# First output projection of a two-layer kernel, computed by column halves around the turn of the state-space result

## What is computed

```python
def even_layer(h, ...):                       # h: 512 tokens x 1024
    ...
    attn = rmsnorm(diff_attention(...), subln_w) * (1.0 - lambda_init)
    y_a = attn.reshape(b, s, 1024) * silu(g_a)
    ...
    y = ssd_scan(xh, dt, A, bm, cm)           # chunks of 128 tokens, 2 groups of 8 heads
    y = (y + xh * d_skip[:, None]).reshape(b, s, 1024) * silu(z)
    y_b = rmsnorm(y in 2 groups of 512, ssd_norm_w)
    return concatenate([y_a, y_b], -1) @ w_out   # w_out: 2048 x 1024
x = x + even_layer(rmsnorm(x, norm_a), ...)
x = x + odd_layer(rmsnorm(x, norm_c), ...)
```

## Time and profile before

| | |
|---|---|
| median of 3 executions | 1669.97 us (1668.33 to 1672.4) |
| the profiled execution's own time | 1672.1 us |
| its span, from the first to the last instruction | 1670.2 us |
| PE busy | 1575.8 us, 94% |
| DVE, ACT, POOL busy | 808.7, 655.9, 244.5 us |
| mean granted PE clock | 0.976 of full |

### The profile page before, as it was taken

How to read it: one execution, slowest core, us unless ns; L and a number is a source line. 1 busy time by engine, 2 the same in 40 slices (tenths; PEclk the granted TensorE clock), 3 DMA queues, 4 the chain that set the end, 5 groups by cost and what they waited for, 6 DMA issues and landing times. The chain is left out here.

```text
span 1670.2 us, 20830 instructions
## 1 busy us (share of the span) xinstructions
PE 1575.8 (94%) x7924; PEld 1287.3 (77%) x7924; DVE 808.7 (48%) x1600; ACT 655.9 (39%) x1324; POOL 244.5 (15%) x148
## 2 busy tenths in 40 slices
PE   7999999899799999998999999988998999999997
PEld 6888777687687879877878777767776888887886
DVE  4222288746723655526723477726654433333224
ACT  4222355552512467625235454453244322222212
POOL 0000022267400011120002223221200000000000
PEclk9999999999899999999999999988999999999999
DMA  5232211111232431122431221112220322322232
GB/s 203 101 102 88 89 51 51 39 51 47 80 101 77 132 102 39 39 84 87 141 96 64 89 70 57 51 52 76 89 76 26 101 90 100 101 89 92 96 100 76
DMA packets 39777, 137.60 MB, mean 82 GB/s; under 512 B 4928, under 2 KB 5312, under 8 KB 39552
## 3 DMA queue, kind: packets, MB, share of 16 engines
q1 hardware_dynamic: 34400, 125.32, 22.7%
q10 hardware_dynamic: 5280, 10.97, 2.2%
HBM read 128.02 MB, written 2.10 MB: 78 GB/s over the span
## 5 line engine op out<-in xcount | busy, mean ns | idle before, releaser
L210 ACT ACTIVATE cut_hi<-raw 128x1024 fp32r<-128x1024 f32 x228 | 241.6, 1060 | 646.8 <-PE ps L227 631.8
L227 PE MATMUL ps<-h_hi,cut_hi 128*128 128x512 f32 (+1 forms) x1120 | 453.0, 404 | 5.9 <-DVE h_lo L425 3.9
L215 DVE TENSOR_TENSOR cut_lo<-raw,cut_hi 128x1024 fp32r<-128x1024 f32 x172 | 211.8, 1231 | 492.0 <-ACT cut_hi L210 490.2
L229 PE MATMUL ps<-h_hi,cut_lo 128*128 128x512 f32 (+1 forms) x1120 | 438.1, 391 | 0.0
L228 PE MATMUL ps<-h_lo,cut_hi 128*128 128x512 f32 (+1 forms) x1120 | 437.8, 391 | 0.0
L227 PEld LDWEIGHTS ps<-h_hi,cut_hi 128*128 128x128 f32 x1120 | 212.5, 190 | 70.0 <-issue 22.9
L229 PEld LDWEIGHTS ps<-h_hi,cut_lo 128*128 128x128 f32 x1120 | 212.1, 189 | 45.6
L228 PEld LDWEIGHTS ps<-h_lo,cut_hi 128*128 128x128 f32 x1120 | 212.9, 190 | 37.6
L215 POOL TENSOR_TENSOR cut_lo<-raw,cut_hi 128x1024 fp32r<-128x1024 f32 x56 | 133.7, 2388 | 675.1 <-ACT cut_hi L210 675.1
L227 PE MATMUL ps<-cut_hi,h_hi 128*128 128x512 f32 (+1 forms) x368 | 143.4, 390 | 10.2 <-DVE cut_lo L215 6.4
L229 PE MATMUL ps<-cut_hi,h_lo 128*128 128x512 f32 (+1 forms) x368 | 142.5, 387 | 0.0
(11 more groups left out here) (312 smaller groups left out, 2103.3 us busy)
## 6 DMA issues: line engine op xcount, KB each, us to landing
raw<-weights SPq DMA_DIRECT2D x228, 512.0 KB, 3.3
scr<-scr ACTq DMA_DIRECT2D x34, 64.0 KB, 3.6
x<-x_in SPq DMA_DIRECT2D x4, 512.0 KB, 6.1
x<-x_in ACTq DMA_DIRECT2D x1, 2048.0 KB, 7.5
q_stack<-qT_lo ACTq DMA_DIRECT2D x16, 128.0 KB, 2.3
out<-x SPq DMA_DIRECT2D x4, 512.0 KB, 2.6
consts<-tables ACTq DMA_DIRECT2D x1, 1732.0 KB, 7.9
arena<-arena ACTq DMA_DIRECT2D x8, 128.0 KB, 2.3
```

What stands on the lines that cost most here:

```text
L210: act.activation(cut_hi[:, u % CUT, :], raw[:, u % RAW, :], ACT.Copy).then_inc(hi_ready, 1)
L215: eng.tensor_tensor(cut_lo[:, u % CUT, :], raw[:, u % RAW, :], cut_hi[:, u % CUT, :].bitcast(F32), ALU.subtract).then_inc(lo_ready, 1)
L227: a = pe.matmul(out, left[0], right[0], start=start, stop=False)
L229: return a, pe.matmul(out, left[1], right[0], start=False, stop=stop)
```

## The change

The parts TurnWaits, GroupMean, turn_a, TurnRead, GroupScale, turn_b, TurnDone and the Combine are replaced by one part, `OutA`, which does the same work in another order:

- The projection is made by column halves. The left 512 columns of all four token tiles need four banks (2, 3, 0, 1), the right 512 the other four (4 to 7). A weight unit now holds two 128-row blocks of one column half instead of one block of both; the host arranges it so. Units 0 to 7 are the left half, 8 to 15 the right.
- y_a is turned through the left banks in two rounds of four blocks. PE no longer waits for the whole scan first.
- The products of the left half start with y_a's blocks. At unit 3 PE turns y_b's blocks 0 to 3 through the right banks, at unit 4 blocks 4 to 7; the left half then goes on with y_b.
- DVE adds the left half to x in the middle of the part, and the right half at the end, with the norm's steps.
- The last two states (i = 6 and 7) are not made: no L1455 product, no weighted input, no forward step.

```diff
-        class TurnWaits(Part):
-
-
-            def pe(self, pe):
-                pe.wait_ge(sl_scaled, NT)
-                pe.wait_ge(y_out, 8)
-                pe.wait_ge(st_out, 8)
-                pe.wait_ge(segs_exp, 16)
-                pe.wait_ge(fill_g.out_act, 8)
...
         def squares_of(act, i):
             c, g = i // 2, i % 2
             act.wait_ge(z_scaled, i + 1)
-            act.wait_ge(st_out, i + 1)
+            if i < 6:
+                act.wait_ge(st_out, i + 1)
...
-                    pe.wait_ge(xdd_ready, i + 1)
-                    if i:
-                        pe.wait_ge(st_out, i)
-                    pe.matmul(ps[:, 6, :], b_tok[:, c, g * P:(g + 1) * P], xdd[i % 2], start=True, stop=True)\
-                      .then_inc(st_done, 1)
+                    if i < 6:
+                        pe.wait_ge(xdd_ready, i + 1)
+                        if i:
+                            pe.wait_ge(st_out, i)
+                        pe.matmul(ps[:, 6, :], b_tok[:, c, g * P:(g + 1) * P], xdd[i % 2], start=True, stop=True)\
+                          .then_inc(st_done, 1)
...
-                act.wait_ge(fill_g.out_act, 8)
-                turn_a.silus(act)
-                squares_of(act, 6)
-                squares_of(act, 7)
...
-                    if c > 0:
+                    if 0 < c < NT - 1:
...
+        class OutA(Part):
...
+            cuts = n - 1
+            after = None
+            left, right = (2, 3, 0, 1), (4, 5, 6, 7)
...
+            def turn(self, pe, y, k, bank, turned):
+                for t in range(NT):
+                    last = pe.transpose(ps[:, bank, t * P:(t + 1) * P], y[:, t, k * P:(k + 1) * P], ident)
+                last.then_inc(turned, 1)
...
+            def columns(self, pe, half, v, order):
+                w = None
+                for k, t in order:
+                    if w is None:
+                        w = unit(pe, self.u0 + v)
+                    y = [(h[:, k % 8, t * P:(t + 1) * P]) for h in ((h_hi, h_lo) if k < 8 else (yb_hi, yb_lo))]
+                    bank = (self.left, self.right)[half][t]
+                    if half == 0 and t == 0:
+                        pe.wait_ge(self.ya_lo_out if k < 8 else self.yb_lo_out, k % 8 + 1)
+                    if half == 0 and k == 0:
+                        pe.wait_ge(self.ya_gated, 4 + t + 1)
+                    if half == 1 and k == 0:
+                        pe.wait_ge(self.yb_lo_out, 4 + t + 1)
+                    a, z = product(pe, ps[:, bank, :], y, [h[:, (k % 2) * 512:(k % 2 + 1) * 512] for h in w],
+                                   k == 0, k == 15)
+                    if (k, t) == order[0]:
+                        first = a
+                    if k == 15:
+                        z.then_inc(self.done, 1)
+                return first
+
+            def pe(self, pe):
+                pe.wait_ge(sl_scaled, NT)
+                pe.wait_ge(fill_g.out_act, 8)
+                for k in range(4):
+                    if k == 2:
+                        pe.wait_ge(segs_exp, 16)
+                    self.turn(pe, y_a, k, self.left[k], self.ya_turned)
+                for k in range(4, 8):
+                    pe.wait_ge(self.ya_gated, k - 3)
+                    self.turn(pe, y_a, k, self.left[k - 4], self.ya_turned)
+                for v in range(8):
+                    if v == 3:
+                        pe.wait_ge(gs_scaled, 5)
+                        pe.wait_ge(gs_scaled_act, 3)
+                        pe.wait_ge(off_read, 6)
+                        pe.wait_ge(y_out, 8)
+                        pe.wait_ge(st_out, 6)
+                        for k in range(4):
+                            self.turn(pe, y_b, k, self.right[k], self.yb_turned)
+                    if v == 4:
+                        for k in range(4, 8):
+                            pe.wait_ge(self.yb_lo_out, k - 3)
+                            self.turn(pe, y_b, k, self.right[k - 4], self.yb_turned)
+                    self.columns(pe, 0, v, [(k, t) for k in (2 * v, 2 * v + 1) for t in range(NT)])\
+                        .then_inc(weights_used, 1)
+                for v in range(8, 14):
+                    self.columns(pe, 1, v, [(k, t) for k in (2 * v - 16, 2 * v - 15) for t in range(NT)])\
+                        .then_inc(weights_used, 1)
+                for t in range(NT):
+                    first = self.columns(pe, 1, 14, [(12, t), (13, t)])
+                    if t == 0:
+                        first.then_inc(weights_used, 1)
+                    first = self.columns(pe, 1, 15, [(14, t), (15, t)])
+                    if t == NT - 1:
+                        first.then_inc(weights_used, 1)
...
             def act(self, act):
-                act.wait_ge(turn_a.turned, 8)
+                act.wait_ge(fill_g.out_act, 8)
+                for k in range(8):
+                    act.activation(gate_a[:, k, :], gate_a[:, k, :], ACT.Silu).then_inc(self.ya_silued, 1)
+                    if k == 3:
+                        squares_of(act, 6)
+                squares_of(act, 7)
+                for k in range(8):
+                    if k == 6:
+                        cut_high(act, self.u0 + 1)
+                    act.wait_ge(self.ya_gated, k + 1)
+                    act.activation(h_hi[:, k, :], gate_a[:, k, :], ACT.Copy).then_inc(self.ya_hi_out, 1)
+                act.wait_ge(self.ya_turned, 8)
                 act.dma_start(x[:, :, :], x_dram.rearrange("(t p) d -> p t d", p=P)).then_inc(x_loaded, 16)
                 act.dma_start(big_row[:, :], big_dram[0, :].partition_broadcast(P)).then_inc(big_loaded, 16)
                 act.wait_ge(gs_rooted, 1)
                 for i in range(5, 8):
                     act.activation(groups_b[:, i, :], groups_b[:, i, :], ACT.Copy, scale=rs[:, i:i + 1])\
                        .then_inc(gs_scaled_act, 1)
-
-            def pe(self, pe):
-                pe.wait_ge(gs_scaled, 5)
-                pe.wait_ge(gs_scaled_act, 3)
-
-        yb = halves("yb", ARENA, ARENA + 4096, 8)
-        turn_b = Turn("yb", lambda t, k: y_b[:, t, k * P:(k + 1) * P], lambda k: (yb[0][:, k, :], yb[1][:, k, :]), 8,
-                      lambda k: col("ssd_norm", k))
-        out_a = Combine("out_a", "out_a", lambda k: (h_hi[:, k, :], h_lo[:, k, :]) if k < 8
-                        else (yb[0][:, k - 8, :], yb[1][:, k - 8, :]), 16, x_back=16, before=turn_b)
+                cut_high(act, self.u0 + 2)
+                cut_high(act, self.u0 + 3)
+                for k in range(8):
+                    if k == 4:
+                        cut_high(act, self.u0 + 4)
+                    act.wait_ge(self.yb_turned, k + 1)
+                    act.activation(yb_hi[:, k, :], ps[:, self.right[k % 4], :], ACT.Copy,
+                                   scale=col("ssd_norm", k)).then_inc(self.yb_hi_out, 1)
+                for v in range(5, self.n):
+                    cut_high(act, self.u0 + v)
...
+            def gate(self, dve, k):
+                dve.wait_ge(self.ya_turned, k + 1)
+                dve.wait_ge(self.ya_silued, k + 1)
+                dve.scalar_tensor_tensor(gate_a[:, k, :], ps[:, self.left[k % 4], :], subln8, gate_a[:, k, :],
+                                         ALU.mult, ALU.mult).then_inc(self.ya_gated, 1)
+
+            def add(self, dve, half, t):
+                dve.wait_ge(self.done, NT * half + t + 1)
+                xv = x[:, t, half * 512:(half + 1) * 512]
+                dve.tensor_tensor(xv, ps[:, (self.left, self.right)[half][t], :], xv, ALU.add)\
+                   .then_inc(self.out_dve, 1)
+
+            def dve(self, dve):
+                for k in range(4):
+                    self.gate(dve, k)
+                dve.wait_ge(sd_squared, 8)
+                dve.tensor_scalar(ms[:, 0:8], ss[:, 0:8], 1.0 / 512, EPS_A, ALU.mult, ALU.add).then_inc(gs_mean, 1)
+                for k in range(4, 8):
+                    self.gate(dve, k)
+                dve.wait_ge(gs_rooted, 1)
+                for i in range(5):
+                    dve.tensor_scalar(groups_b[:, i, :], groups_b[:, i, :], rs[:, i:i + 1], None, ALU.mult)\
+                       .then_inc(gs_scaled, 1)
+                    if i == 2:
+                        cut_low(dve, self.u0 + 1)
+                cut_low(dve, self.u0 + 2)
+                cut_low(dve, self.u0 + 3)
+                for k in range(8):
+                    if k == 4:
+                        cut_low(dve, self.u0 + 4)
+                    dve.wait_ge(self.yb_hi_out, k + 1)
+                    dve.scalar_tensor_tensor(yb_lo[:, k, :], ps[:, self.right[k % 4], :], col("ssd_norm", k),
+                                             yb_hi[:, k, :].bitcast(F32), ALU.mult, ALU.subtract)\
+                       .then_inc(self.yb_lo_out, 1)
+                for v in range(5, 9):
+                    cut_low(dve, self.u0 + v)
+                dve.wait_ge(x_loaded, 16)
+                for t in range(NT):
```

(62 more changed lines are left out.)

17 lines of the change are left out of this document (2 added, 15 removed).

## The result

| | before | changed |
|---|---|---|
| median of 4 executions each, this comparison | 1669.95 us (1668.33 to 1672.40) | 1655.14 us (1650.92 to 1658.06) |
| ratio | | 0.9909, 95% interval 0.9888 to 0.9931 |
| profiled execution: its time, its span | 1672.1, 1670.2 us | 1650.9, 1648.6 us |
| mean granted clock of the profiled execution | 0.976 | 0.988 |
| mean of all executions whose clock is on record | 1667.7 us (73), clock 0.9785 | 1657.3 us (16), clock 0.9823 |

The changed kernel is faster, by 14.8 us in the first comparison and by 10.4 (plus or minus 2.1, two standard errors of the means) over all executions of both kernels. The first lies outside the forecast: 7.0 us less, range 1659.5 to 1666.5. The second does too if only the time is taken, but as a saving it lies at the range's fast end, since 1670.0 - 1659.5 is 10.5.

The account below looks back on a forecast made before the run. PE's waits and slow clock were taken as the bound. Start 13.9, less y_b's turn 3.7, seams 0.5, clock 2.5 and tail 0.2, gave 7.0 us less: 1670.0 to 1663.0 us, range 1659.5 to 1666.5.

Parts of the forecast that it names:

- the start: First projection product at 437.7 instead of 451.58: 13.9 us earlier, range 12.5 to 14.2.
- the last states: Not making them in the scan buys nothing by itself; it keeps DVE's gates from pushing the power back 1.7 us.
- What was added: Between first product and end: y_b's 32 transposes, now inside the projection, 3.7 us, and seams 0.5; projection matmuls cost 0.
- The seams: Four changes between products and transposes on PE: 0.5 us, bounds 0 and 1.0.
- The tail: End of the projection, where epsilon and scaling follow the last add: 0.2 us cost, bounds 0 and 0.7.
- The clock at the place: First projection products run at half clock, as in the second layer: 2.5 us lost, bounds 0 and 4.8.
- rival 1: At the start of the projection the clock does not fall: saving 9.5 us, time 1660.5, chance 14%.
- the clock elsewhere: Everything before 420 and after the norm only shifted; about 1 us allowed for the spread of a median of three.
- The hidden steps: Each moved step during the projection is ready before PE needs it; y_b's scaling has 10.7 us of cover.
- Unit 1's low half: Cut in 1.53 us beside POOL, done at 443.0; PE needs it at 445.6 with the dip, 443.1 without.
- Rival 2: The dip at the projection's start lasts longer, 10.4 us: saving 4.7, time 1665.3, chance 12%.
- Rivals 3 and 4: 3: y_b unready for its turn at unit 3, 1670, 5%. 4: left half at half clock over four banks, 1698, 3%.

Follow-up runs that it names:

- states_only: The kernel before, without the last two states: 1665.33 us, ratio 0.9992.
- with_states: The changed kernel, with the last two states made as before: 1659.69 us.
- the faster version: The changed kernel with POOL's first two low halves ahead of the power, and other steps moved earlier: 1652.75 us (0.9902), again 1652.41 (0.9908).
- wait_scaled: The changed kernel, but PE waits for y_b's first three scaled pieces before its first product: 1660.56 us (0.9951).
- turn_first: The changed kernel with its column halves, but y_b turned in both rounds ahead of the first product: 1665.66 us, ratio 0.999.

## Why the prediction was wrong

- **What bounds it, and the start: right.** The first product came 13.7 us nearer to the scan's last group, and that group 0.6 earlier, together 14.3 where I had 13.9, just above my range of 12.5 to 14.2. The gates ran from 429.49, the power from 432.36, the first low half from 433.96, each in the order and at the distance of the working. That the last states buy nothing by themselves was right as well (states_only, 0), and that making them here would push the first product back too (with_states, 1.2 us where I had 1.7).
- **What was added: slightly too much.** From the first product to the last it takes 92.2 us instead of 88.6, so y_b's turn costs 3.6, not 3.7 + 0.5. The seams cost nothing. The tail cost 0.2, as in the sum.
- **The clock at the place: the step of the sum that failed.** I charged 2.5 us for a dip over the first products and called its absence rival 1, with 14%. The size was right (2.9, 2.4 and, for a short one, 1.6 us), the odds were not: two of the three profiles of the changed kernel had no dip. I had leaned on the second layer, whose turn is followed by 3.81 us of idle PE; here the pauses are 1.9 and 2.4, with the short turns between them, and the same program falls on either side from one execution to the next. What decides between them stays open. Without the term the sum would have been 9.5, and with the seams and the start as measured 10.4. The place shows 10.5 without a dip and 7.6 with it. That the mean over all executions is 10.4 too is in part luck: it holds executions with the dip, and others with a better clock elsewhere.
- **What I treated as fixed: the clock elsewhere.** I wrote that stages before and after would be as they were, only shifted, and gave 1 us for the spread of a median. The kernel before alone goes from 1660.2 to 1672.7 us, the slower executions with the lower mean clock. This step took the result out of the range: with a sum of 10.4 the forecast would have been 1659.6, just inside it, and the medians of four lay another 4.4 us apart, which was luck. The range should have had some 3 us on both sides for that instead of 1. Even then 1659.6 - 3 = 1656.6 would have missed the measured 1655.1, by 1.5.
- **The hidden steps: all hidden, one barely.** y_b was ready for both rounds without a wait, x too. Unit 1's low half took 2.31 us beside POOL, not 1.53, and ended at 440.64 for a unit that PE needed near 440.8. My row for it was a cut beside POOL too, and this one took 0.8 us longer; unit 2's took 2.31 as well, still beside POOL, and unit 3's 1.23, with POOL through (at 443.44 and 447.92, POOL's last subtraction ending at 446.89). What sets the length beside POOL is not shown. Where the first product is early and the clock full, this cut is next in line, which is why the faster version moves it ahead.
- **The rivals.** Rival 1 happened, mostly. Rival 2 is seen in one form: a stretch of 10.2 us fell across the start once, but 4.4 us of it lay over the turn and a pause, so it cost 2.9. Rivals 3 and 4 did not: no new wait at unit 3, and the clock held 1.00 over four banks (435.3 to 527.9 in the windows above) as it had over eight. That four banks could keep it at 0.50 was a conjecture of mine; no run shows it.

## What to carry to other kernels

In these runs a pause could come with two prices, its length and a stretch at clock 0.50 near it (2.9 us in the changed kernel's third profile, 2.4 in wait_scaled), and the second was paid in one of three profiles of the changed kernel: look at several profiles of one program before charging it or leaving it out. Compare two kernels at a place by distances between their own instructions, not by spans; here one program's spans differed by 12 us with the place the same to 0.5. And when a long wait is to be filled, look for the first instruction that truly needs the late value: here POOL's power could go behind the first two low halves.

## What the runs showed of the hardware

- The stretches at half clock differ between executions of one program. Within its span, by the granted clock, the kernel before had 79.5 us of them in one profile and 47.9 in another, with spans of 1670.2 and 1658.5; the changed kernel 40.8, 62.2 and 68.6 in three, with spans of 1648.6, 1655.5 and 1658.6. Whole stretches of 10 us come and go (1085.5 to 1096.0 above, clock 0.51 in one profile of the kernel before and 1.00 in the other). The two spans of the kernel before are 0.7% apart.
- Idle transposes of a constant in pauses of 2.8 and 7.4 us went with a clock of 1.00 there and delayed nothing (one profile). The whole kernel before gained 2.3 us by them, barely clear of the noise (0.9986, 0.9974 to 0.9999); on the changed kernel, 1.0 us was not clear of it.
- The clock fell during short transposes behind a pause of 1.9 us in three profiles (the changed kernel's third, turn_first, the faster version's second; 16 transposes took 3.28, 3.24 and 3.15 us) and did not fall there in four with the same pause (the changed kernel's first two, wait_scaled, the faster version's first; 2.63 us each). It held once over 2.8 us, in the kernel before with idle transposes.
- DVE's subtraction of 1024 elements, both operands in SBUF, takes 1.23 us alone. Beside POOL's subtractions it took 2.31 here, 1.53 in the second layer and 1.43 in wait_scaled. POOL's own go from 1.35 us each to 12.93/8 = 1.6.
